# Forgetting heads' keys in the first attention steps, early gate rows, raw latents turned, X and the unit matrix first

## The chip, the cores and the metric

The kernel runs on one core of one Trainium2 chip. The time of a run is the device time of one execution in microseconds; of the kernel before three runs are given. Beside them stands one profiled execution, whose times of instructions and transfers are quoted below. The device time is a little longer than the span from the first to the last profiled instruction.

## What is computed

Three transformer layers in a row on 256 tokens of 1024 channels, all in fp32. Cut to its outline:

```
x = x + diff_attention(rms_norm(x) ...)        # 8 heads, two softmax maps each, head norm, w_out
x = x + hier_moe(rms_norm(x) ...)              # router, 64 experts (1024 -> 256 -> 1024), top 2
x = x + mla_attention(rms_norm(x) ...)         # latents: a = h @ w_a; rms_norm(cq) @ w_qb, rms_norm(ckv) @ w_kvb
x = x + hier_moe(rms_norm(x) ...)              # 64 other experts
mod = silu(c) @ w_ada + b_ada                  # sh1, sc1, ga1, sh2, sc2, ga2
x = x + ga1 * hybrid_mixer(modulate(rms_norm(x), sh1, sc1))   # 8 sliding heads, 8 forgetting heads
x = x + ga2 * conv_glu_mlp(modulate(rms_norm(x), sh2, sc2))
return rms_norm(x) * g_final
```

A forgetting head adds the difference of cumulated log sigmoids to its scores; a sliding head adds a slope by distance and a sink.

## The kernel before

Tokens stand in two tiles of 128. The kernel is written by hand: each engine has its own program in the order in which its lines call it, and semaphores join them (the blocks `sync`, `gpsimd`, `scalar`, `vector` and `tensor` at the end). SyncE's queue issues nearly all weight transfers, in units of 1 MB, into a ring of 12 slots and, for the experts, 4 more slots in the buffer BC; a unit's transfer waits until TensorE has released the slot (`load_unit` L230, `load` of the experts L1584).

The stages and their names: norm `n1`, projection `p1` (L486), turn `t1` (L556), first attention `a1` with output product `o1`; experts `m1`; norm `n2`, latents `pa`, turn of the latents `t3`, projections `pq` and `pkv` with the head norms of `heads_vector`, turns `t4q` and `t4k`, second attention `a2` with `o2`; experts `m2`; norm `n3`, projection `pz`, the channels `channels_tensor` (L1862), attention `a3` with `o3`; norm `n4` and the MLP (L2084, L2099).

`attention_stage` goes through 16 steps, 8 head pairs of the first token tile and 8 of the second. In step i TensorE forms the scores of step i+2 or i+3 (L627), turns the probabilities of step i (L638), does what the stage puts beside it, and multiplies with the values (L650). VectorE masks and stores (L684, L718), ScalarE takes the exponential (L744) and copies the turned map (L755). Beside them:

- A filler: in `a1` the products of the conditioning vector (L966), one unit in each of the first 8 steps. ScalarE copies the result (L978) and sends it to DRAM (L980) in step 7, and TensorE waits for that copy (`bank_read`) at the end of step 7.
- `OutStage`: in the second half of the steps TensorE multiplies the first tile's heads with w_out, in 16 pieces (L391), so many in each step as `counts` says, after the heads have been turned (L363) and ScalarE and VectorE have copied them (L372, L376). The second tile's product (L403) comes after the stage; the next norm's turn (L272) stands between its halves. VectorE adds the product to X (`add`).

The experts' transfers begin when the attention before has stored its last head (`x_free`); they pass some 200 MB per layer. At the latents, ScalarE copies a (L1648) and squares it (L1658), GpSimd takes the roots (L1668), VectorE scales the latents (L1674) and TensorE then turns them (L556). The head norms' VectorE loop starts with L1750.

In the third layer `channels_tensor` forms seven groups f = 0 to 6 of keys and queries; groups 5 and 6 are the keys of the forgetting heads, which steps 4 to 7 and 12 to 15 use. The rows of the first gate ga1 and their bias are loaded by GpSimd (L2013, L2014) after `a3` has stored its last head, and added by VectorE (L2018):

```
        def gate1_gpsimd(pool):
            a3.ready(pool)
            gate_gpsimd(pool, 0)
```

At the start TensorE waits for the unit matrix and both norm gains (`first`), which stand in SyncE's queue behind X.

Of the kernel before, what the change touches and what calls it, by code (L numbers as in the profile page):

```python
# [14 lines left out]
P = 128  # L15
# [86 lines left out]
def build(nc, t, out):  # L102

    with ExitStack() as ctx:
# [212 lines left out]
        def close_vector(dve, products, norm):  # L317
            products.add(dve, 0, 0)
# [13 lines left out]
        def close_vector_late(dve, products, norm):  # L332
            products.add(dve, 0, 0)
# [12 lines left out]
        class OutStage:  # L346
# [37 lines left out]
            def pieces(self, pe, first, last):  # L384

                for k in range(first, last):
                    g, n, c = k // 8, k // 4 % 2, 4 * (k // 8) + k % 4
                    self.heads_in(pe, 0, c)
                    u, view = self.blocks[n][1][g][0:2]
# [27 lines left out]
            def tensor(self, pe, i, heads_ready):  # L417

                if self.heads_norm:
# [4 lines left out]
                    counts = (0, 0, 0, 3, 3, 3, 2, 1)  # L424
# [21 lines left out]
            def vector(self, dve, i):  # L446
# [145 lines left out]
        def attention_stage(name, ready, heads, scale, bias, out, filler=None, mix=False, sink=0, squares=None,  # L592
                            turned_in=pT, heads_ready=None):
# [23 lines left out]
            def tensor(pe):  # L617
                ready(pe)

                def score(i):  # L620
                    tt, h, w = place(i)
                    if i >= ahead:
                        pe.wait_ge(*masked(maps * (i - ahead + 1)))
                    for m in range(maps):
# [31 lines left out]
                if filler:  # L656
                    filler.tensor(pe, 0)
                for i in range(items):
# [17 lines left out]
            def vector(dve):  # L676
# [48 lines left out]
                for i in range(items):  # L725
# [4 lines left out]
                    if i + 1 < items:  # L730
                        weigh(i + 1)
                    out.vector(dve, i)
# [3 lines left out]
            def scalar(act):  # L736
# [22 lines left out]
                for i in range(items):  # L759
# [3 lines left out]
                    if filler and i < HEADS:  # L763
                        filler.scalar(act, i)
                    if squares and i >= 1:
# [16 lines left out]
        def start_sync(sp):  # L782
# [35 lines left out]
        N_SMALL = 16 * 23  # L818
        first = sem("first")
        N_FIRST = 16 * 3  # L820
        x_in = [sem(f"x_in{tt}") for tt in range(TT)]

# [10 lines left out]
        n1 = norm_stage(lambda eng, tt: eng.wait_ge(*x_in[tt](16)), gains[:, 0, 0, :], extra=[(first, N_FIRST)],  # L833
# [816 lines left out]
        a_sq, a_rs, a_scaled = shared("sum_sq", 4), shared("sum_rs", 2), shared("sum_out", 2)  # L1650
# [676 lines left out]
```

## Time and profile before

| | us |
|---|---|
| median of 3 runs | 1658.75 (1657.42 to 1659.88) |
| profiled execution | 1659.99 |
| its span | 1658.3 |
| TensorE busy in it | 1378.7 (83%) |
| VectorE, ScalarE, GpSimd busy | 565.6, 260.4, 102.6 |
| mean granted TensorE clock | 0.921 of 2.4 GHz |
| bytes moved | 512.76 MB |

The span divides thus: the first attention up to its last stored head 0 to 152; experts 152 to 646; latents and second attention up to the last stored head 764; experts to 1255; hybrid attention to 1418; MLP to the end. The profiled execution is 1.2 us above the median. Busy shares of TensorE count an instruction at 1.2 GHz as busy for twice as long as at 2.4.

### The profile page before, as it was taken

Reading aid. Unit: us, or ns where it says so; the run is one execution under the profiler, and the core shown is the slowest. Engines: PE = TensorE matmul, PEld = TensorE weight load, DVE = VectorE, ACT = ScalarE, POOL = GpSimd, SP = SyncE. Lnnn points to the kernel's source line nnn. Section 1 sums busy time; section 2 is a strip of 40 time slices with the busy share of each in tenths; the row PEclk is TensorE's granted clock in tenths of the full one; section 3 lists DMA queues with packets and bytes.
Section 4 is the critical chain, followed back from the end, with each engine's and each line's share of the span. In section 5 each row is a group of like instructions: output and inputs, shape, how many; then the busy total and the mean of one; then the engine's idle time right before and its main releaser. Section 6 shows DMA issues by size and latency. Waiting matters only on the chain.

```text
span 1658.3 us, 24316 instructions
## 1 busy us (share of the span) xinstructions
PE 1378.7 (83%) x9354; PEld 840.2 (51%) x9354; DVE 565.6 (34%) x1490; ACT 260.4 (16%) x736; POOL 102.6 (6%) x191
## 2 busy tenths in 40 slices
PE   7989998677676667879997776767768988999998
PEld 3445555344443343555563443434435865788843
DVE  3444543122122222562632221222213133477721
ACT  2143211001010011353110010100101032111100
POOL 1312000000000001210100000000000032000000
PEclk9998999888898899999998888988988979999999
DMA  8763999999999999615999999999999512444400
GB/s 296 286 248 139 396 422 420 421 421 422 422 422 422 422 421 386 205 52 215 415 420 421 421 422 421 422 422 422 422 421 360 163 52 79 165 152 153 152 0 26
DMA packets 117188, 512.76 MB, mean 309 GB/s; under 512 B 11856, under 2 KB 46604, under 8 KB 64888
## 3 DMA queue, kind: packets, MB, share of 16 engines
q1 hardware_dynamic: 115504, 507.56, 77.0%
q0 software_dynamic: 1584, 4.13, 0.7%
q8 instruction: 51, 0.84, 0.2%
q14 instruction: 25, 0.20, 0.0%
q10 hardware_dynamic: 24, 0.02, 0.0%
HBM read 510.61 MB, written 1.07 MB: 309 GB/s over the span
## 4 chain that ended last, share of the span: by engine, by line
PE 33%; DMA 13%; SPq 6%; DVE 3%; issue 1%; ACT 1%; POOL 0%; DVEq 0%; POOLq 0%; ACTq 0%
DMA ring<-in_moe_w_up 13%; PE bank L2084 9%; SPq L1584 6%; PE bank L2099 5%; PE bank L1184 4%; PE bank L1862 3%; PE bank L391 2%; PE bank L650 1%; PE bank L403 1%; PE bank L1170 1%; PE bank L1199 1%; PE bank L627 1%; PE bank L486 1%; PE bank L1212 1%; PE bank L638 1%
## 5 line engine op out<-in xcount | busy, mean ns | idle before, releaser
L1184 PE MATMUL bank<-ring,hT 128*32 128x256 f32 (+1 forms) x3072 | 235.1, 463 | 161.3 <-DMA ring<-in_moe_w_up 106.2
L1184 PEld LDWEIGHTS bank<-ring,hT 128*32 128x32 f32 (+1 forms) x3072 | 136.6, 133 | 269.7 <-issue 236.1
L1435 DVE TENSOR_SCALAR pT<-pT 128x256 f32<-128x256 f32 x34 | 10.0, 294 | 475.4 <-ACT pT L1551 475.4
L2084 PE MATMUL bank<-hT,ring 128*128 128x256 f32 (+1 forms) x736 | 152.7, 370 | 1.7 <-ACT hT L285 1.7
L2084 PEld LDWEIGHTS bank<-hT,ring 128*128 128x128 f32 x736 | 134.9, 190 | 19.1 <-DVE hT L290 1.8
L486 PE MATMUL bank<-ring,hT 128*128 128x512 f32 (+4 forms) x352 | 124.7, 517 | 8.8 <-DVE hT L288 3.9
L1170 PE MATMUL bank<-A,hn 128*128 128x128 f32 x1088 | 127.8, 276 | 0.7 <-DVE A L1356 0.7
L1184 PE MATMUL bank<-BC,hT 128*32 128x256 f32 (+1 forms) x1024 | 85.9, 476 | 50.8 <-DMA BC<-in_moe_w_up 30.0
L1170 PEld LDWEIGHTS bank<-A,hn 128*128 128x128 f32 x1088 | 125.1, 193 | 3.2 <-issue 3.2
L1212 PE MATMUL bank<-A 128*128 128x512 f32 x256 | 118.4, 605 | 0.0
L486 PEld LDWEIGHTS bank<-ring,hT 128*128 128x128 f32 x352 | 65.8, 198 | 65.7 <-issue 53.1
L1184 PEld LDWEIGHTS bank<-BC,hT 128*32 128x32 f32 (+1 forms) x1024 | 48.8, 139 | 90.9 <-issue 78.8
L1199 PE MATMUL bank<-ring,gtab 128*32 128x512 f32 (+1 forms) x768 | 94.7, 595 | 0.0
L1551 ACT ACTIVATE pT<-bank 128x256 f32<-128x256 f32 x34 | 13.0, 383 | 513.6 <-PE bank L1184 513.6
L1212 PEld LDWEIGHTS bank<-A 128*128 128x128 f32 x256 | 46.0, 189 | 59.0 <-issue 59.0
L2099 PE MATMUL bank<-ring,BC 128*128 128x512 f32 x176 | 75.7, 592 | 0.0
L1378 DVE TENSOR_TENSOR hT<-bank,gains 128x512 f32<-128x512 f32 x34 | 23.5, 692 | 136.7 <-PE bank L1170 136.7
L256 POOL TENSOR_SCALAR stat<-stat 128x1 f32<-128x1 f32 x12 | 2.3, 190 | 986.5 <-ACT hn L249 986.5
L1436 DVE RECIPROCAL pT<-pT 128x256 f32<-128x256 f32 x34 | 59.6, 1753 | 1.2
L1540 ACT ACTIVATE hT<-bank,gains 128x128 f32<-128x128 f32 x136 | 38.7, 367 | 118.0 <-PE bank L1170 118.0
L2099 PEld LDWEIGHTS bank<-ring,BC 128*128 128x128 f32 x176 | 33.5, 190 | 41.6 <-issue 41.6
L1199 PEld LDWEIGHTS bank<-ring,gtab 128*32 128x32 f32 (+1 forms) x768 | 24.9, 112 | 49.5 <-issue 38.6
(289 smaller groups left out, 1478.5 us busy)
## 6 DMA issues: line engine op xcount, KB each, us to landing
ring<-in_moe_w_gate SPq DMA_DIRECT2D x100, 1024.0 KB, 24.8
ring<-in_moe_w_down SPq DMA_DIRECT2D x96, 1024.0 KB, 26.6
ring<-in_moe_w_up SPq DMA_DIRECT2D x92, 1024.0 KB, 26.6
BC<-in_moe_w_up SPq DMA_DIRECT2D x36, 1024.0 KB, 26.8
BC<-in_moe_w_down SPq DMA_DIRECT2D x32, 1024.0 KB, 26.2
BC<-in_moe_w_gate SPq DMA_DIRECT2D x28, 1024.0 KB, 26.1
ring<-in_w_ada SPq DMA_DIRECT2D x24, 1024.0 KB, 5.8
ring<-in_w_up SPq DMA_DIRECT2D x22, 1024.0 KB, 5.3
```

The costliest lines, as they stand in the source:

```text
L391: i = nc.tensor.matmul(bank[2 + n][:, :], hT[:, c, 0:P], view(slot(u))[:, c % 4, :], start=(c == 0), stop=(c == DC - 1))
L486: i = nc.tensor.matmul(ps(n, tt)[:, 0:w], lhs(seen + c, tt), view(slot(u))[:, c, :], start=(seen + c == 0), stop=(seen + c == total - 1))
L1170: i = nc.tensor.matmul(TOKENS[c // 4][:, c % 4 * P:(c % 4 + 1) * P], tokens_by_channel[:, tt, c, :], hot[:, tt, :], start=(tt == 0), stop= ...
L1184: i = nc.tensor.matmul(GATE[q * cap:(q + 1) * cap, part * FF:(part + 1) * FF], xg[:, c, q * cap:(q + 1) * cap], u[:, c, :], start=(c == 0) ...
L1199: i = nc.tensor.matmul(SIDE[nb][q * cap:(q + 1) * cap, :], hidT[:, c, q * cap:(q + 1) * cap], u[:, c, nb * NB:(nb + 1) * NB], start=(c == ...
L1212: i = nc.tensor.matmul(bank[2 * tt + nb][:, :], share[:, tt * P:(tt + 1) * P], yrow[:, nb * NB:(nb + 1) * NB], start=first, stop=False)
L1436: wait(nc.vector.reciprocal(e, e))
L1540: i = nc.scalar.activation(xg[:, c, :], TOKENS[1][:, (c - 4) * P:(c - 3) * P], ACT.Identity, scale=gain[:, c:c + 1])
L1584: sp.dma_start(slot(u), expert_src).then_inc(unit_full[s].sem, 16)
L1862: i = nc.tensor.matmul(bank[(2 + f) % 4][:, b * S:(b + 1) * S], w[:, c, b * P:(b + 1) * P], hT[:, c, :], start=(c == 0), stop=(c == DC - 1))
L2084: i = nc.tensor.matmul(bank[n % 4][:, b * S + t0:b * S + t1], w[:, c, b * P:(b + 1) * P], hT[:, c, t0:t1], start=(c == 0), stop=(c == DC - 1))
L2099: i = nc.tensor.matmul(bank[4 + 2 * tt + n][:, :], hidT3[:, 2 * j + c, tt * P:(tt + 1) * P], w[:, c, n * NB:(n + 1) * NB], start=(j == 0 a ...
```

## The change

- SyncE's queue begins with the unit matrix and X's first tile, then the attention gains and two weight units, then X's second tile. The FFN gains come after four units. TensorE waits for the unit matrix and X's first tile alone, and multiplies a cleared part of hT twice before that.
- `a1`: the pieces of the first tile's product are spread as (2, 2, 0, 2, 2, 2, 1, 1) in place of (0, 0, 0, 3, 3, 3, 2, 1); TensorE waits for the copy of the conditioning row in step 10 in place of step 7.
- The first `add` of each output product is done in step 15 of the attention.
- The latents are turned as they are; the root is applied in ScalarE's copies of the products (L1700 and following). VectorE's `latent_vector` is gone.
- Groups 5 and 6 of the channels are formed in four blocks, one before step 0 and one in each of steps 0 to 2 of `a3`; `channels_evac` of them stands in ScalarE's step 0 and VectorE's step 2.
- The first gate's rows and the convolution's are loaded before `bias_gpsimd`, in other places of BC, and added by VectorE before `a3`.

```diff
@@ OutStage.tensor, vector; close_vector
-        def close_vector(dve, products, norm):
-            products.add(dve, 0, 0)
+        def close_vector(dve, products, norm, first_added=True):
+            if not first_added:
+                products.add(dve, 0, 0)
...
-                    counts = (0, 0, 0, 3, 3, 3, 2, 1)
+                    counts = (2, 2, 0, 2, 2, 2, 1, 1)
...
+                if i == 2 * HEADS - 1:
+                    self.add(dve, 0, 0)
@@ attention_stage
+                    if beside:
+                        beside.keys_ready(pe, i)
...
+                if beside:
+                    beside.tensor(pe, 0)
...
-                    if filler and i + 1 == HEADS:
+                    if filler and i == HEADS + 2:
                         filler.bank_read(pe)
+                    if beside:
+                        beside.tensor(pe, i + 1)
@@ start_sync
-            for tt in range(TT):
-                ld(X[:, tt, :], x[:, tt, :], x_in[tt])
-            ld(ident, t["constants"][:, 0:P], first)
+            ld(ident, t["constants"][:, 0:P], x_in[0])
+            ld(X[:, 0, :], x[:, 0, :], x_in[0])
             ld(gains[:, 0, :, :], t["attn_norm"].rearrange("l (p c) -> p l c", c=DC), first)
-            ld(gains[:, 1, :, :], t["ffn_norm"].rearrange("l (p c) -> p l c", c=DC), first)
-            for u in range(4):
+            for u in range(2):
                 load_unit(sp, u)
+            ld(X[:, 1, :], x[:, 1, :], x_in[1])
+            for u in range(2, 4):
+                load_unit(sp, u)
+            ld(gains[:, 1, :, :], t["ffn_norm"].rearrange("l (p c) -> p l c", c=DC))
@@ the latents
-        t3 = turn_stage("t3", lambda pe: pe.wait_ge(*a_scaled(1)),
+        t3 = turn_stage("t3", lambda pe: pe.wait_ge(*pa.copied(2)),
...
-                        fill_ready=lambda pe, f: pe.wait_ge(*a_scaled(1 if f == 0 else 2)))
+                        fill_ready=lambda pe, f: pe.wait_ge(*pa.copied(2 if f == 0 else 4)))
...
+            eng.wait_ge(*a_rs(1))
+            return nc.scalar.activation(q_l[:, tt, 2 * n:2 * n + 2, :], ps.rearrange("p (h d) -> p h d", h=2), ACT.Copy,
+                                        scale=stat[:, 448 + tt:449 + tt])
@@ the hybrid attention
+        class ForgetKeys:
+            def tensor(self, pe, i):
+                if i < 4:
+                    f = 5 + i // 2
+                    if i % 2 == 0:
+                        z_left(pe, f - 4 if f == 5 else 4)
+                    channel_block(pe, f, i % 2)
+            def scalar(self, act, i):
+                if i == 0:
+                    channels_evac(act, 5)
+            def vector(self, dve, i):
+                if i == 2:
+                    channels_evac(dve, 6)
+            def keys_ready(self, pe, h):
+                if h == SWA_PAIRS:
+                    z_left(pe, 5)
+                if h == SWA_PAIRS + 2:
+                    z_left(pe, 6)
...
-            z_left(pe, 5)
-            z_left(pe, 6)
+            z_left(pe, 3)
+            z_left(pe, 4)
...
-            a3.ready(pool)
+            m2.ready(pool, 1)
             gate_gpsimd(pool, 0)
...
+            gate1_gpsimd(pool)
             bias_gpsimd(pool)
-            gate1_gpsimd(pool)
@@ vector, tensor
+            nc.vector.memset(hT[:, 0:2, :], 0.0).then_inc(cleared.sem, 1)
...
             forget_vector(dve)
+            gate_vector(dve, 0)
             a3.vector(dve)
-            gate_vector(dve, 0)
...
-            pe.wait_ge(*first(N_FIRST))
+            pe.wait_ge(*cleared(1))
+            for _ in range(2):
+                nc.tensor.matmul(bank[7][:, :], hT[:, 0, 0:P], hT[:, 0:2, :].rearrange("p c s -> p (c s)"), start=True, stop=True)
```

How the change moves instructions is shown at three places; the rows stand in each engine's own order.

SyncE at the very start, before (X, the unit matrix as konst, gains, weight units as ring):

```order
L785 DMA X<-in_x 128x1024 x2
L785 DMA konst<-in_constants 128x128
L785 DMA gains<-in_attn_norm 128x2x8
L785 DMA gains<-in_ffn_norm 128x2x8
L230 DMA ring<-in_diff_w_in 128x4x512 x4
```

and now:

```order
L801 DMA konst<-in_constants 128x128
L801 DMA X<-in_x 128x1024
L801 DMA gains<-in_attn_norm 128x2x8
L230 DMA ring<-in_diff_w_in 128x4x512 x2
L801 DMA X<-in_x 128x1024
L230 DMA ring<-in_diff_w_in 128x4x512 x2
L801 DMA gains<-in_ffn_norm 128x2x8
```

The first unit stands behind three transfers in place of five, and the second tile of X behind two units.

TensorE from the spreading of the gates (L1949) into the steps of `a3`, before (L1862 channels, L627 scores, L638 turn, L650 product with the values):

```order
L1949 MATMUL bank<-A,konst 128x256 x8
L1862 MATMUL bank<-hT,ring 128x256 x32
L627 MATMUL bank<-BC 128x128 x6
L638 MATMUL bank<-konst,BC 128x128 x2
L650 MATMUL bank<-A,BC 128x64 x2
L627 MATMUL bank<-BC 128x128 x2
L638 MATMUL bank<-konst,BC 128x128 x2
L650 MATMUL bank<-A,BC 128x64 x2
```

and now (the same lines are L1996, L1875, L635, L646, L658):

```order
L1996 MATMUL bank<-A,konst 128x256 x8
L635 MATMUL bank<-BC 128x128 x4
L1875 MATMUL bank<-hT,ring 128x256 x8
L635 MATMUL bank<-BC 128x128 x2
L646 MATMUL bank<-konst,BC 128x128 x2
L1875 MATMUL bank<-hT,ring 128x256 x8
L658 MATMUL bank<-A,BC 128x64 x2
L635 MATMUL bank<-BC 128x128 x2
L646 MATMUL bank<-konst,BC 128x128 x2
L1875 MATMUL bank<-hT,ring 128x256 x8
L658 MATMUL bank<-A,BC 128x64 x2
```

The 32 matmuls that stood ahead of all scores stand in four blocks of 8, the first behind the scores of steps 0 and 1, the others between turn and product of steps 0, 1 and 2.

GpSimd in the third layer, now (constants for `a3`, then the gate rows from mod_scratch and b_ada, the convolution's rows, and then the first biases; before, the four rows from mod_scratch to in_conv_b stood behind all biases):

```order
L1944 DMA A<-in_constants 128x128
L1945 DMA A<-in_constants 128x384
L2060 DMA BC<-mod_scratch 128x1024
L2061 DMA BC<-in_b_ada 128x1024
L2103 DMA BC<-in_conv_w 44x128 x3
L2104 DMA BC<-in_conv_b 44x128
L2037 TENSOR_SCALAR BC<-A 128x128 x8
```

Six DMA issues were moved ahead of the biases of the 16 steps.

## Rows read from the trace of the kernel before

**Rows 1.** The page's 40 slices of the span: DMA share in tenths

```profile
DMA  8763999999999999615999999999999512444400
```

**Rows 2.** Timeline of the first 40 us: start us, us, engine, line, operation, idle before it

```profile
6.86 1.97 PE L272 MATMUL bank<-konst,X 128*128 128x128 f32 x8 [6.86 <-DMA gains<-in_ffn_norm]
...
10.32 8.70 PE L486 MATMUL bank<-ring,hT 128*128 128x512 f32 x16 [1.49 <-DMA ring<-in_diff_w_in]
```

**Rows 3.** Line L230 in the first 12 us: its four weight units

```profile
DMA to landing us min/median/max: 7.0/10.2/13.4
```

**Rows 4.** Timeline of the first attention, steps 7 and 8, several engines

```profile
123.15 1.06 ACTq L980 DMA_DIRECT2D mod_scratch<-modrow  x1
123.18 1.11 PE L363 MATMUL bank<-konst,hn 128*128 128x128 f32 x4 [1.98 <-ACT modrow L978]
...
124.62 0.67 ACT L372 ACTIVATE hT<-bank,small 128x512 f32<-128x512 f32 x1
```

**Rows 5.** Windows: TensorE busy, weight loads, VectorE, ScalarE, GpSimd, clock, DMA share, GB/s

```profile
50.00:80.00 30.00, 30.00 (x71) 13.31 (x70) 14.85 (x27) 4.60 (x8) 10.08 (x9) 1.00 0.70 269
...
122.00:124.00 2.00, 0.82 (x4) 0.82 (x5) 0.68 (x2) 1.12 (x5) 0.00 (x0) 0.69 1.00 422
...
136.00:138.00 2.00, 2.00 (x8) 1.07 (x7) 1.50 (x7) 1.24 (x5) 0.03 (x1) 0.90 0.00 0
```

**Rows 6.** Timeline: scores in steps 12 and 13, first expert transfers, second tile's product

```profile
139.68 0.70 PE L627 MATMUL bank<-BC 64*128 64x256 f32 x4
...
143.71 0.70 PE L627 MATMUL bank<-BC 64*128 64x256 f32 x4
...
152.56 1.06 SPq L1584 DMA_DIRECT2D BC<-in_moe_w_gate  x2
...
155.85 7.03 PE L403 MATMUL bank<-ring,hT 128*128 128x512 f32 x16
```

**Rows 7.** Timeline of the latents, from ScalarE's second copy to the head norms

```profile
673.19 0.73 ACT L1648 ACTIVATE hn<-bank,stat 128x192 f32<-128x192 f32 x2 [2.78 <-PE bank L486]
...
676.62 1.55 PE L556 MATMUL bank<-konst,hn 128*128 128x128 f32 x6 [3.02 <-DVE hn L1674]
...
678.75 13.42 PE L486 MATMUL bank<-ring,BC 128*128 128x384 f32 x35 [0.58 <-DVE BC L572]
...
686.38 0.55 DVE L1750 TENSOR_REDUCE stat<-hn 128x2 f32<-128x384 f32 x1 [7.01 <-ACT hn L1726]
...
690.51 0.55 DVE L1750 TENSOR_REDUCE stat<-hn 128x2 f32<-128x384 f32 x1
```

**Rows 8.** Window of 1 us there, columns as in rows 5

```profile
682.00:683.00 1.00, 1.00 (x4) 0.55 (x3) 0.00 (x0) 0.00 (x0) 0.00 (x0) 0.73 0.00 0
```

**Rows 9.** TensorE's timeline from the last channel groups to step 9 of the hybrid attention

```profile
1323.00 15.77 PE L1862 MATMUL bank<-hT,ring 128*128 128x256 f32 x64
...
1345.40 1.11 PE L650 MATMUL bank<-A,BC 128*128 128x64 f32 x4 [0.47 <-ACT BC L755]
...
1348.34 1.11 PE L650 MATMUL bank<-A,BC 128*128 128x64 f32 x4 [0.47 <-ACT BC L755]
...
1369.59 0.70 PE L627 MATMUL bank<-BC 64*128 64x256 f32 x4
```

**Rows 10.** Windows of 1 us: hybrid attention's begin; second attention's steps, columns as in rows 5

```profile
1344.00:1345.00 1.00, 0.93 (x7) 0.50 (x6) 0.59 (x4) 0.73 (x6) 0.92 (x3) 0.87 0.02 8
...
730.00:731.00 1.00, 0.76 (x6) 0.76 (x7) 0.22 (x2) 0.57 (x3) 0.00 (x0) 1.00 0.00 0
```

**Rows 11.** Timeline of the hybrid attention's end: gate rows, adds, norm

```profile
1395.60 0.60 POOL L2013 DMA_DIRECT2D A<-mod_scratch  x1 [14.70 <-DVE hn L718]
...
1401.17 1.23 DVE L2018 TENSOR_TENSOR A<-A 128x1024 f32<-128x1024 f32 x1 [3.26 <-DMA A<-in_b_ada]
...
1408.21 1.97 PE L272 MATMUL bank<-konst,hn 128*128 128x128 f32 x8 [4.16 <-DVE hn L262]
1409.98 8.53 PE L403 MATMUL bank<-ring,hT 128*128 128x512 f32 x16
```

More of the change, by code:

```diff
@@ L330, in close_scalar, with close_vector_late @@
                 norm.evac(act, tt, 1)
-        def close_vector_late(dve, products, norm):
-            products.add(dve, 0, 0)
+        def close_vector_late(dve, products, norm, first_added=True):
+            if not first_added:
+                products.add(dve, 0, 0)
             products.add(dve, 0, 1)
@@ L592, in attention_stage @@
         def attention_stage(name, ready, heads, scale, bias, out, filler=None, mix=False, sink=0, squares=None,
-                            turned_in=pT, heads_ready=None):
+                            turned_in=pT, heads_ready=None, beside=None):
             st = Stage()
@@ L731, in vector @@
                         weigh(i + 1)
+                    if beside:
+                        beside.vector(dve, i)
                     out.vector(dve, i)
@@ L764, in scalar @@
                         filler.scalar(act, i)
+                    if beside:
+                        beside.scalar(act, i)
                     if squares and i >= 1:
@@ L816, in start_sync @@
             assert n_loaded[0] == N_SMALL
-        N_SMALL = 16 * 23
+        N_SMALL = 16 * 24
         first = sem("first")
-        N_FIRST = 16 * 3
+        N_FIRST = 16
         x_in = [sem(f"x_in{tt}") for tt in range(TT)]
+        cleared = sem("cleared")
         w_in = t["diff_w_in"][0]
@@ L831, in have_small @@
             eng.wait_ge(*loaded(N_SMALL))
-        n1 = norm_stage(lambda eng, tt: eng.wait_ge(*x_in[tt](16)), gains[:, 0, 0, :], extra=[(first, N_FIRST)],
+        n1 = norm_stage(lambda eng, tt: eng.wait_ge(*x_in[tt](16 * (2 - tt))), gains[:, 0, 0, :], extra=[(first, N_FIRST)],
                         late_root=True)
@@ L1850, in z_left, with channel_bank, channel_block @@
             eng.wait_ge(*(z_out_a if f % 2 else z_out_v)(f // 2 + 1))
+        def channel_bank(f):
+            return bank[(2, 3, 0, 1, 2, 3, 2)[f]]
+        def channel_block(pe, f, b):
+            u = turned_units[f]
+            unit_here(pe, u)
+            w = wide_unit(slot(u))
+            for c in range(DC):
+                i = nc.tensor.matmul(channel_bank(f)[:, b * S:(b + 1) * S], w[:, c, b * P:(b + 1) * P],
+                                     hT[:, c, :], start=(c == 0), stop=(c == DC - 1))
+            if f == 0 or b == 1:
+                i.then_inc(unit_done.sem, 1)
         def channels_tensor(pe):
-            for f, u in enumerate(turned_units):
+            for f in range(5):
                 if f < 4:
@@ L1857, in channels_tensor @@
                     z_left(pe, f - 4)
[L1858 to L1859 removed]
                 for b in range(1 if f == 0 else 2):
[L1861 to L1864 removed]
+                    channel_block(pe, f, b)
                 if f in (2, 3, 4):
                     (forget_sums, forget_turn, forget_spread)[f - 2](pe)
+        class ForgetKeys:
[16 more added lines that the diff above has]
+                    z_left(pe, 6)
+        forget_keys = ForgetKeys()
         def channels_evac(eng, f):
             eng.wait_ge(*unit_done(turned_units[f] + 1))
[L1870 removed]
+            ps = channel_bank(f)
             copy = (lambda dst, src: nc.scalar.activation(dst, src, ACT.Copy)) if f % 2 else nc.vector.tensor_copy
@@ L2022, in add @@
                 xs = X[:, tt, n * NB:(n + 1) * NB]
-                product = scratch[k][:, n * NB:(n + 1) * NB]
+                product = scratch[k][n]
                 dv.done(nc.vector.tensor_tensor(product, ps, gate_rows[k][:, n * NB:(n + 1) * NB], ALU.mult))
@@ L2239, in _ @@
             forget_scalar(act)
-            for f in (1, 3, 5):
+            for f in (1, 3):
                 channels_evac(act, f)
```

43 lines of the change are left out of this document (15 added, 28 removed).

## The prediction, on record before the change was timed

> **What bounds the kernel now.** I read the page's slices first. The DMA queues are full in slices 5 to 16 and 20 to 30, the two expert layers [rows 1]: there the 200 MB of a layer set the end, and nothing that TensorE does faster is worth time. Outside them, from 10 to 152 us, from 646 to 764 and from 1255 to the end, the DMA rows are low and TensorE's timeline is nearly closed. So a microsecond taken from TensorE's order before 152 or 764 counts if it lets the expert transfers start earlier. They start right behind the last stored head: the first issue is at 152.56 [rows 6], and the DMA queues stand idle before it. So I read the chain of waits of these three stretches and the granted clock beside it, and look in each for gaps of TensorE and for work at 1.2 GHz in place of 2.4.
>
> **The change part by part**, summed against the profiled execution (1659.99, 1.2 above the median).
>
> *Start.* TensorE begins at 6.86, released by the FFN gains, and the first product at 10.32, released by a weight unit [rows 2], which needs 7.0 us from its issue to its landing [rows 3]. The unit is now issued behind three small or half-size transfers and not five, two issues of about 0.45 us each earlier, and has 0.5 MB less ahead of it, some 1.2 us at about 400 GB/s. I take 2.0 us. X's first tile and the turn come sooner still and no longer bound it. The first product's 16 records take 8.70 us, where the same 16 take 7.03 later [rows 2, 6]: the clock is at 1.2 GHz in the beginning, which costs 1.7. The two products on cleared data warm it, but then TensorE waits again for the unit; I count half, 0.8. Start: −2.8, bounds 0 and −4.5. The projection behind it leaves TensorE no gap (30.00 us busy of 30 from 50 to 80 [rows 5]), so this goes through.
> The Trainium skill, "TensorE: Matmul & The Clock Gate", section "HAM oscillation — how this bites in real kernels", and its first part say that the low clock is spent by time at work and not by the number of matmuls, and that a gap can bring it back. By the first half of that alone this term would be −3.7 and the sum 28.7; no row here shows a warmed start.
>
> *First attention.* In step 7 TensorE stands 1.98 us for ScalarE's copy of the conditioning row [rows 4]; by the shares of two windows the clock falls at 122.8 and comes back at 136.4 [rows 5]. That wait moves to step 10, where the copy is long done. But what is late next stands in the same queue: ScalarE issues a transfer (1.06 us from 123.15) and copies the turned heads only until 125.3 [rows 4]. The pieces, now in step 8, wait for that copy, about 2.0 us from 123.3. From there at 2.4 GHz: a step with three pieces takes 4.03 [rows 6], a piece 7.03/8 = 0.88, so a step with two takes 3.15. Step 8 ends at 127.6, step 9 at 130.8, step 10 (no piece, but the turn of four heads) at 133.0; step 13 begins at 139.3 and not at 143.71. From there to the first expert transfer it was 8.85; two pieces fewer make 7.1, so 146.4: −6.1. As the gap is as long as before, the clock most likely falls again, now with TensorE closed behind it, so for 4 to 5 us: +2.3. I take −3.8, bounds 0 (the gap only moves and the clock stays down as before) and −6.1. The `add` put into VectorE's step 15 (0.7 us) fits ahead of the last head's product and costs nothing; without that cover, 0.7.
>
> *Latents.* ScalarE's second copy ends at 673.92; TensorE turns only at 676.62, after 3.02 us for squares, root and scaling, and pq begins at 678.75 [rows 7]. Now the turn goes at 674.1, its copies end at about 675.8, and pq begins at 675.9. The clock falls in that gap and returns at 682.5, by the window's share [rows 8]. So pq's first block ran 3.8 us at half clock; its 12 records, 384 columns wide, take 0.33 each at 2.4 GHz (three quarters of 7.03/16), 3.9 in all, and 5.8 with the low stretch, to 684.6. With the clock kept it ends at 679.8. VectorE's loop, begun at 686.38 and then closed at 4.13 per round [rows 7], sets the end of this stage; it begins 5.0 earlier with the clock kept and 2.9 earlier without. The two gaps left (0.5 and 1.0) speak for kept more often than not: −4.5. The scale in ScalarE's copies is free: L1648 has one too.
>
> *Hybrid attention.* The last two groups run as one stretch of 15.77 until 1338.8, and step 9 begins at 1369.59: 30.8 us for steps 0 to 8 [rows 9]. The clock falls at 1344.7 [rows 10], and a step then takes 2.94, 0.47 of it waiting [rows 9]. In the new order TensorE first waits 0.8 for the last copies of the forget rows, and forms two scores (0.7). Steps 0 to 2 have a block of 3.9 each between turn and product and so no gap: 1.33 each of their own, 4.0. Steps 3 to 7 are open: 2.47 of work at 1.2 GHz is 1.23 at 2.4, and with waits 2.0 each, the last two with wider scores 2.2: 10.4. Step 8 with eight turns 2.95. Together 18.9, so −11.9 with the clock kept. It was kept in the second attention at 0.76 busy [rows 10], about what these steps have. I take off 2 for the copies of both groups, which stand in ScalarE's step 0 and VectorE's step 2 ahead of the next copy and store: −10, bounds −5 (clock down from step 4 to 8) and −11.9. Queues: GpSimd has six more issues, 3.7 us, in the 55 us in which it waits before its first bias; VectorE's gate addition (1.23) [rows 11] delays mask 0, covered by the first block. The 1 MB more of transfers then go beside weights for which TensorE doesn't wait; without that slack 3 us.
>
> *Gate rows.* After the last head GpSimd issues them at 1395.60, VectorE adds them at 1401.17, and TensorE, done with its product at 1404.05, turns at 1408.21 after 4.16 idle, at half clock [rows 11]: 8 turns take 1.97 for 1.05, the next product 8.53 for 7.03. All of it goes: without the load the chain of add, square, root and scale ends at 1402.4, before the product. −4.2 −0.9 −1.5 = −6.6; bounds −5 and −7. Late next is the second tile's chain, as before.
>
> Sum: −2.8 −3.8 −4.5 −10 −6.6 = −27.7. 1659.99 − 27.7 = 1632.3; 1.2 lower against the median, **1631**.
>
> **Rivals.** *B: the clock falls again in the open steps.* For it: it fell in this very attention after gaps of under 1 us [rows 10], and it fell at each gap of 2 us or more that I read closely. Against: the second attention's steps. Price: the hybrid term at its bound, 5 less, and the latents at theirs, 1.6 less: 1638. The page named above says the same in general: without activity TensorE is throttled.
>
> *C: what lies before the expert layers is hidden by them.* The next transfers after the first four wait for slots that the output product frees. If these set the pace, the start, first attention and latents (11.1) are lost: 1642. Against it: the product follows the last head at the same distance, so the slots move along, and the queues are idle before 152.56 [rows 6].
>
> *D: slower.* The four blocks go into a stretch whose clock was low. If it falls at the steps' begin and the steps keep it down, the blocks take 31.5 and not 15.8, and the second eight steps with their pieces, some 26 us at 2.4 GHz, as long again: +15.7 + 26, and the gain of 10 is gone: 1631 + 52 = 1683. It decides from the point where the first scores of the stage run at 1.2 GHz and no later product lifts them. Against it: the clock came back before step 9 once TensorE was closed, and a step with a block is closed.
>
> *E: the change doesn't do what it says*, as when a wait of a later semaphore sends TensorE to the same place: no gain, 1659. The order of the instructions shows the blocks and loads moved.
>
> **How the numbers follow.** Forecast (clock kept in most open stretches) 0.5; B 0.35; C 0.08; D 0.03; E and the rest 0.04. The range: down to 1625, where all terms but one stand at their far bounds (−33 to −34); up to 1645, which takes in B with a start and a first attention at little, and C. Faster means by over 0.2%, 3.3 us, about what a measurement here can tell: forecast, B and C, and some of the rest, 0.95; same 0.02; slower 0.03.
>
> **What would show it.** In the profile of the changed kernel: the first L492 product near 8.3; the first expert transfer near 146; 0.5 us of gap before the latents' second turn and the first round of the head norms 9 to 12 us earlier than 686 in all; the clock at 2.4 in steps 3 to 7 of the hybrid attention; no gap of TensorE between the two halves of its output product. I am wrong if the expert layers take longer than before, if a gap of 2 us or more stands ahead of the pieces in every attention, or if the hybrid steps 3 to 7 take 2.9 each.

## The result, and the profile after

The changed kernel takes 1633.12 us (median of 4 runs, 1631.00 to 1634.69); the kernel before, beside it on the same chip, 1659.32. The ratio is 0.9838, with a 95% interval of 0.9821 to 0.9855: 26 us faster, where 28 were forecast. The profiled execution took 1634.69, the slowest of the four; its span is 1632.9 (before 1658.3), TensorE's mean granted clock 0.930 (before 0.921), the bytes are the same 512.76 MB.

The page's slices of the span, clock and DMA share in tenths:

```profile
PEclk9999999888898898999999898898888989999999
DMA  8765999999999999615999999999999721644400
```

The full slices of the two expert layers are as many as in [rows 1], but a slice of 41 us can't size changes of a few. So I cut each trace at four marks that stand in every kernel and compare the pieces: TensorE's turn of X's second tile (start), the issue of the first expert transfer (first attention), that of the second layer's (experts and latents), and GpSimd's first root of the third norm (experts).

| stretch (us) | before | after | moved | forecast |
|---|---|---|---|---|
| to the second turn | 18.86 | 19.87 | +1.0 | −2.8 |
| to the first expert transfer | 133.70 | 127.88 | −5.8 | −3.8 |
| to the second layer's | 611.29 | 606.16 | −5.1 | −4.5 (latents) |
| to the third norm's root | 495.56 | 494.69 | −0.9 | 0 |
| to the end | 398.89 | 384.30 | −14.6 | −16.6 (hybrid, gates) |

TensorE's timeline of the start, and two windows of it (columns as in rows 5):

```profile
1.55 3.78 PE L2326 MATMUL bank<-hT 128*128 128x512 f32 x4 [1.55 <-DVE hT L2297]
5.25 1.16 PE L272 MATMUL bank<-konst,X 128*128 128x128 f32 x8
10.24 9.79 PE L492 MATMUL bank<-ring,hT 128*128 128x512 f32 x16 [3.84 <-DMA ring<-in_diff_w_in]
```

```profile
9.00:10.00 1.00, 0.00 (x0) 0.00 (x0) 0.00 (x0) 0.00 (x0) 0.00 (x0) 0.50 1.06 412
15.00:16.00 1.00, 1.00 (x2) 0.27 (x1) 0.00 (x0) 0.27 (x2) 0.56 (x2) 0.67 1.06 391
```

The two products at 1.55 do raise the clock: the turn takes 1.16 and not 1.97 [rows 2]. But the first weight unit, issued at 2.24, releases TensorE at 10.24, as late as before, and in the 3.84 us of waiting the clock falls again. It is back only in the window 15 to 16, and the first product takes 9.79, more than the 8.70 of [rows 2].

The first attention, TensorE and SyncE's queue, and a window in the gap:

```profile
123.79 0.44 PE L646 MATMUL bank<-konst,BC 128*128 128x128 f32 x2
126.36 1.99 PE L395 MATMUL bank<-ring,hT 128*128 128x512 f32 x4 [2.13 <-ACT hT L374]
147.75 0.85 SPq L1603 DMA_DIRECT2D BC<-in_moe_w_gate  x2
```

```profile
125.00:126.00 1.00, 0.00 (x0) 0.00 (x0) 0.49 (x2) 0.67 (x3) 0.18 (x1) 1.00 0.99 418
```

The gap of [rows 4] has moved one step on and is as long as before, but here the clock holds through it: two pieces take 1.99.

The latents (TensorE, then VectorE's head norms):

```profile
668.44 1.18 PE L562 MATMUL bank<-konst,hn 128*128 128x128 f32 x6 [0.37 <-ACT hn L1667]
670.19 15.75 PE L492 MATMUL bank<-ring,BC 128*128 128x384 f32 x48 [0.58 <-DVE BC L578]
676.13 0.55 DVE L1765 TENSOR_REDUCE stat<-hn 128x2 f32<-128x384 f32 x1 [5.33 <-ACT hn L1741]
```

The gap of 3.02 in [rows 7] is 0.37, and VectorE's loop begins 10.25 us earlier, at 676.13.

The hybrid attention, from its first scores to step 9, and its end:

```profile
1312.81 1.23 PE L635 MATMUL bank<-BC 64*128 64x128 f32 x8 [0.88 <-DVE A L1969]
1313.97 4.78 PE L1875 MATMUL bank<-hT,ring 128*128 128x256 f32 x16
1319.37 3.62 PE L1875 MATMUL bank<-hT,ring 128*128 128x256 f32 x16
...
1333.92 0.66 PE L658 MATMUL bank<-A,BC 128*128 128x64 f32 x4 [0.47 <-ACT BC L769]
...
1335.85 0.66 PE L658 MATMUL bank<-A,BC 128*128 128x64 f32 x4 [0.47 <-ACT BC L769]
1336.43 0.67 PE L635 MATMUL bank<-BC 64*128 64x128 f32 x4
...
1341.55 1.11 PE L658 MATMUL bank<-A,BC 128*128 128x64 f32 x4 [0.47 <-ACT BC L769]
...
1350.92 0.70 PE L635 MATMUL bank<-BC 64*128 64x256 f32 x4
...
1378.36 7.03 PE L407 MATMUL bank<-ring,hT 128*128 128x512 f32 x16
1385.23 1.05 PE L272 MATMUL bank<-konst,hn 128*128 128x128 f32 x8
1386.12 7.03 PE L407 MATMUL bank<-ring,hT 128*128 128x512 f32 x16
```

and a window in step 5:

```profile
1336.00:1337.00 1.00, 1.00 (x8) 0.74 (x8) 0.29 (x1) 0.56 (x4) 0.92 (x2) 0.81 0.94 316
```

A block takes 3.62 and covers a step's waits; the first takes 4.78, as the clock was down from about 1312.7 to 1316. The open steps 3 and 4 (products 1333.92 and 1335.85) run at 2.4 GHz, 1.93 apart; at about 1336.6 the clock falls. Counted from the scores at their begin, step 5 takes 2.80, the steps 6 and 7 take 3.36 each, and step 8 with its eight turns takes 4.97, together 14.49. Step 9 begins at 1350.92, 18.7 us earlier than in [rows 9], 11.1 of which was won before the stage. The end has no gap where [rows 11] had 4.16, and the second half of the product takes 7.03 and not 8.53: from the last turn of heads (1377.92; 1396.59 before) to the MLP's first matmuls (1393.08; 1418.44 before) it is 15.2 for 21.9.

### The profile page after: what moved, and what is told of

The parts are those of the page before. It is cut to its first block, busy times and chain, and to the rows that moved or that the text cites. A ratio compares the mean times of both kernels' runs of the same rounds, so it can differ in the third digit from the quotient of the medians.

```text
span 1632.9 us, 24329 instructions
## 1 busy us (share of the span) xinstructions
PE 1367.9 (84%) x9358; PEld 833.6 (51%) x9358; DVE 564.5 (35%) x1487; ACT 263.2 (16%) x736; POOL 103.5 (6%) x191
## 2 busy tenths in 40 slices
DMA packets 117188, 512.76 MB, mean 314 GB/s; under 512 B 11856, under 2 KB 46604, under 8 KB 64888
## 4 chain that ended last, share of the span: by engine, by line
PE 35%; DMA 11%; SPq 7%; DVE 2%; issue 1%; ACT 1%; POOL 0%; POOLq 0%; DVEq 0%; ACTq 0%
DMA ring<-in_moe_w_up 11%; PE bank L2131 9%; SPq L1603 6%; PE bank L2146 5%; PE bank L1203 4%; PE bank L1875 3%; PE bank L1189 2%; PE bank L1218 2%; PE bank L395 2%; PE bank L407 2%; PE bank L1231 2%; PE bank L635 1%; PE bank L492 1%; PE bank L658 1%; PE bank L646 1%
## 5 line engine op out<-in xcount | busy, mean ns | idle before, releaser
L1203 PE MATMUL bank<-ring,hT 128*32 128x256 f32 (+1 forms) x3072 | 243.0, 476 | 162.2 <-DMA ring<-in_moe_w_up 100.8
L492 PE MATMUL bank<-ring,hT 128*128 128x512 f32 (+4 forms) x352 | 125.4, 519 | 11.1 <-DVE hT L288 3.9
L1203 PE MATMUL bank<-BC,hT 128*32 128x256 f32 (+1 forms) x1024 | 76.8, 434 | 49.8 <-DMA BC<-in_moe_w_up 32.6
```

Of the source, the lines that this page charges most:

```text
L492: i = nc.tensor.matmul(ps(n, tt)[:, 0:w], lhs(seen + c, tt), view(slot(u))[:, c, :], start=(seen + c == 0), stop=(seen + c == total - 1))
L1203: i = nc.tensor.matmul(GATE[q * cap:(q + 1) * cap, part * FF:(part + 1) * FF], xg[:, c, q * cap:(q + 1) * cap], u[:, c, :], start=(c == 0) ...
```

## The experiments

All are edits of the changed kernel except `before_fill`. The table has each trace cut at the same marks; the last column is the median of the runs (4 each, `before_fill` 10). The runs come from four groups on two chips; the kernel before, timed again in each, had medians of 1659.3, 1657.5, 1659.9 and 1658.0, so a difference of under 2 us between two medians says little.

| kernel | second turn | to 1st transfer | to 2nd | to root | to end | median |
|---|---|---|---|---|---|---|
| before | 18.86 | 133.70 | 611.3 | 495.6 | 398.9 | 1659.3 |
| before_fill | 20.96 | 132.41 | 610.5 | 494.0 | 393.4 | 1652.9 |
| after | 19.87 | 127.88 | 606.2 | 494.7 | 384.3 | 1633.1 |
| u_ends | 19.38 | 129.50 | 606.3 | 494.9 | 391.4 | 1642.2 |
| u_keys | 17.57 | 127.87 | 606.5 | 494.1 | 396.9 | 1643.6 |
| u_latents | 17.63 | 129.51 | 611.1 | 494.2 | 386.0 | 1638.0 |
| u_counts | 16.86 | 131.22 | 608.3 | 494.9 | 384.6 | 1638.1 |
| u_read | 15.48 | 128.93 | 606.1 | 494.1 | 386.0 | 1635.6 |
| bridge | 17.64 | 129.56 | 606.3 | 494.5 | 384.2 | 1633.7 |
| late_row | 20.02 | 126.44 | 606.1 | 496.1 | 384.5 | 1632.5 |
| fill | 17.51 | 129.51 | 604.3 | 494.3 | 380.6 | 1629.4 |
| ahead_fill | 20.30 | 127.86 | 606.5 | 494.5 | 383.5 | 1634.2 |
| joined | 16.53 | 126.43 | 605.9 | 494.2 | 379.7 | 1624.6 |
| joined_spread | 16.96 | 126.41 | 606.7 | 494.7 | 379.2 | 1624.5 |

**Undoing parts.** `u_ends`: the old order of loads and no early products; the gates' loads and VectorE's sum behind the attention, and with them the hybrid attention's first `add`. Of its edit, the line of the gates:

```diff
-            gate1_gpsimd(pool)
             bias_gpsimd(pool)
+            gate1_gpsimd(pool)
```

> The changed kernel with both its ends undone: SyncE's old order at the start and no products ahead of the first turn; the gate rows loaded after the last head and added to VectorE's work behind the attention. By the traces (start 1.0 us worse with the change, gates 6.7 better): 1633.1 - 1.0 + 6.7 = 1638.8, and the second turn at 18.9 us as before the change. By the forecast's terms (start 2.8 better, gates 6.6): 1642.5.

Measured 1642.21 (ratio to before 0.9893, 0.9876 to 0.9909). That is the 1642.5 of the forecast's terms, but not for their reasons, as the start shows. The gap is back in TensorE's timeline, and with it 7.1 us in the last column:

```profile
1391.14 1.97 PE L272 MATMUL bank<-konst,hn 128*128 128x128 f32 x8 [4.12 <-DVE hn L262]
```

The start is 0.5 better than in the one trace of after. The rest of the 8.5 us between the two traces is in the first attention: the same gap of 2.13 cost the clock here, and its stretch is 129.50 for 127.88. So the gates with that `add` are worth 7, and one trace doesn't size the start.

`u_keys`: `for f in range(7)` in `channels_tensor`, and nothing beside the attention.

> The changed kernel with the last two groups of keys formed ahead of the hybrid attention again, in one stretch, as before the change; the rest stays. Theory (the blocks fill the gaps of the first steps and keep the clock up through the first five of them): step 9 begins 7.5 us later than in the changed kernel, 1640.6. Rival (the hybrid stage won by what else changed there: the add in VectorE's last step, fewer waits ahead of the first scores): under 3 us, 1636. If the clock happens to fall later in the open steps than it did in the one trace of before: 1638.

Measured 1643.62, 10.5 more than after and 3.0 more than expected. In the last column it is 12.6 more; the clock fell at about 1330.6 and came back only at about 1361, in the steps with pieces, later than in the kernel before (windows):

```profile
1360.00:1361.00 1.00, 1.00 (x2) 0.34 (x1) 0.56 (x3) 1.00 (x4) 0.92 (x3) 0.50 0.00 0
1361.00:1362.00 1.00, 1.00 (x3) 0.38 (x2) 0.00 (x0) 0.54 (x3) 0.77 (x2) 0.84 0.00 0
```

Confirmed in kind; the size depends on when the clock returns.

`u_latents`: VectorE scales, and the turn waits for it.

> The changed kernel with the latents scaled by VectorE before they are turned, as before the change. Theory (the 2.6 us chain of squares, root and scaling and the clock that fell in its gap): the second attention's first expert transfer comes 4.4 us later, and as the expert layer behind it only shifts, 1637.5. If the clock holds through the 3 us of gap this time: 2.9 us, 1636. Rival (the expert layer's transfers take up what is won ahead of them): 1633.

Measured 1637.98, where 1637.5 was expected; the column that holds the latents is 611.1, that of before to 0.2 us. (In the traces with the new order of the latents it lies between 604.3 and 608.3.) The expert layer behind it takes as long as ever (494.2), so the rival that transfers hide the gain is out. TensorE's timeline, with the gap of [rows 7]:

```profile
670.48 1.49 PE L562 MATMUL bank<-konst,hn 128*128 128x128 f32 x6 [3.01 <-DVE hn L1693]
672.55 11.87 PE L492 MATMUL bank<-ring,BC 128*128 128x384 f32 x28 [0.58 <-DVE BC L578]
```

`u_counts` and `u_read` take apart the first attention's change:

```diff
-                    counts = (2, 2, 0, 2, 2, 2, 1, 1)
+                    counts = (0, 0, 0, 3, 3, 3, 2, 1)
```
```diff
-                    if filler and i == HEADS + 2:
+                    if filler and i + 1 == HEADS:
```

> The changed kernel with the pieces of the first attention's output product spread as before, (0, 0, 0, 3, 3, 3, 2, 1); TensorE's wait for the conditioning row stays in step 10. Measured from TensorE's turn of X's second tile to the first expert transfer, the kernel before took 133.7 us, the changed one 127.9 where its clock held and 129.5 where it fell in the gap of 2.13. Theory (the three steps without pieces leave TensorE open after the filler has ended, and that kept the clock down before): 131 to 133, so 1635 to 1637. Rival (the wait in step 7 alone brought it down; without it and without pieces that wait for the heads' copy there is no gap of 2 us at all): 126.5 to 128, 1632.

> The changed kernel with TensorE's wait for the conditioning row back in step 7, the pieces spread as now. The heads are then turned 1.5 us later, but ScalarE copies them only behind the row's transfer anyway. Theory (the gap only moves from step 8 to step 7 and the pieces behind it close TensorE either way): the stretch from the second turn to the first expert transfer is 127.9 or 129.5 us as in the changed kernel, at most 1 more, 1633 to 1634. Rival (the gap in step 7 weighs more, as in the kernel before): 131 to 133, 1636 to 1638.

Measured 1638.08 and 1635.61, 1.1 and 1.6 us above their theories, the second close to its rival's 1636. The stretches, 131.22 and 128.93, say what the medians blur (their runs lie 6.5 and 5.8 us apart), and both are where the theory put them. Without pieces in steps 8 to 10 the wait moves to the product of step 8, the clock falls at about 124.5 and the open steps behind it run at 1.2 GHz (TensorE's timeline of `u_counts`):

```profile
123.64 0.71 PE L658 MATMUL bank<-A,pT 128*128 128x128 f32 x4 [2.42 <-ACT pT L769]
124.28 1.08 PE L635 MATMUL bank<-BC 64*128 64x256 f32 x4
...
126.45 1.23 PE L658 MATMUL bank<-A,pT 128*128 128x128 f32 x4 [0.47 <-ACT pT L769]
```

With the wait back in step 7 the clock falls as well, but pieces follow, it is back at 124, and the stretch is no longer than in other traces with a fall. So the spread of the pieces carries 1.7 to 3.3 us of this part; moving the wait gave nothing measurable once they are spread, as ScalarE's row and its transfer stay ahead of the heads' copy. The 1.2 to 2.5 us between `u_counts` and the two traces with the old attention (132.41 and 133.70) are left to the moved wait and the early `add`; no run parts these two.

The four medians with a part undone lie 9.1, 10.5, 4.9 and 5.0 us above that of after, 29.5 in all where the whole change gave 26.2: the parts account for the gain, and their sum is no closer than the runs scatter.

**The start.** `bridge` adds, behind `n1.turn(pe, 0)`:

```diff
+            for _ in range(4):
+                nc.tensor.matmul(bank[0][:, :], ident, X[:, 0, 0:NB], start=True, stop=True)
```

> The changed kernel (1633.1) with four products of the unit matrix with X's first tile behind the first turn, in the 3.84 us in which TensorE stands for the first weight unit. Theory (the two products at the very start raise the clock and the gap behind the turn drops it again, so the first projection product runs at 1.2 GHz for longer than it did before the change): the clock stays at 2.4, the first product takes 7.0 to 7.3 us in place of 9.8, the second turn comes 2.5 to 2.8 us earlier, and the time is 1630.4. Rival (the weight units and X's second tile set the pace of the first 20 us): under 1 us is won, 1632.5. If a clock once raised at 1.5 us doesn't hold through four short products either: no gain, 1633.1 or up to 1 more.

TensorE's timeline, start and first attention:

```profile
6.12 3.60 PE L2329 MATMUL bank<-X,konst 128*128 128x512 f32 x8
10.69 7.11 PE L492 MATMUL bank<-ring,hT 128*128 128x512 f32 x16 [0.98 <-DMA ring<-in_diff_w_in]
...
124.11 3.68 PE L395 MATMUL bank<-ring,hT 128*128 128x512 f32 x4 [2.13 <-ACT hT L374]
```

The mechanism held: 7.11 for the product, the turn 2.2 earlier, though the unit landed late. The median did not move (1633.72, where 1630.4 was expected). The trace shows one reason: in this execution the clock fell in the attention's gap, two pieces took 3.68, and the stretch is 1.7 longer than in the one trace of after.

How much the start varies shows in a trace of another kernel with the changed start (`fill`), where the unit landed 1.4 us earlier and the clock was soon back (timeline):

```profile
8.87 8.80 PE L492 MATMUL bank<-ring,hT 128*128 128x512 f32 x16 [2.43 <-DMA ring<-in_diff_w_in]
```

Over all traces the second turn came at 18.86, 20.96 and 19.38 with the old order (mean 19.7) and at 15.48 to 20.30 with the new one (8 traces, mean 18.2); bridged at 17.64, 16.53 and 16.96 (17.0). In `u_read`, the 15.48, the unit was there before the copies, the gap was 1.35 and the clock was up in the whole product (7.11); there the turn had still taken 1.97, at 1.2 GHz. So the two early products raise the clock at the turn in some executions only: it takes 1.15 to 1.97 over the eight.

**The first attention's gap.** `late_row` puts ScalarE's copy of the conditioning row and its transfer behind `out.scalar(act, i)` in step 7.

> The changed kernel with ScalarE's copy of the conditioning row and its transfer put behind the copy of the turned heads in step 7 of the first attention. TensorE stood 2.13 us for that copy of the heads, and in three of four traces with this very gap the clock fell in it or right behind it for about 3 us. Theory: the gap shrinks to 0.5 us, the clock stays in every execution, the first expert transfer is issued at 145 to 146 in place of 147.0 to 147.75, and the time is 1.6 us shorter than an execution whose clock held, 3 us shorter than one whose clock fell: 1630.5. Rival (VectorE's or the next exponentials' chain is as late as that copy): nothing won, 1633.

TensorE's timeline in step 8:

```profile
124.73 1.98 PE L395 MATMUL bank<-ring,hT 128*128 128x512 f32 x4 [0.35 <-ACT hT L374]
```

The gap is 0.35, the stretch 126.44: 1.4 shorter than 127.9, 3.1 shorter than 129.5. The median, 1632.50, gained only 0.6 and is 2 above the expected 1630.5, less than its runs differ (5.0); in the profiled run the second expert layer took 1.5 us longer than in the others, which I can't explain. In `joined` and `joined_spread` the stretch is 126.4 again.

**The open steps.** `fill` adds to `ForgetKeys.tensor`, for steps 3 to 7:

```diff
+                elif i <= 8:
+                    for _ in range(2):
+                        nc.tensor.matmul(bank[3][:, 0:P], ident, ident, start=True, stop=True)
```

> The changed kernel with two products of the unit matrix with itself (128 columns) between turn and product of each of the steps 3 to 7 of the hybrid attention; their results are read by nobody. Theory (the clock falls because the open steps leave TensorE idle for a quarter of the time): the clock stays, the steps 5 to 8 take 2.0 to 2.3 us in place of 3.4, step 9 begins 4 to 5.5 us earlier, 1628 to 1629. Rival (the clock falls there whatever small work is added, or the waits on ScalarE and VectorE set the step): the ten products cost up to 0.45 us each time two of them don't fit in a gap, 1633 to 1636.

TensorE's timeline, the first block and steps 7 to 9, and a window of these:

```profile
1310.95 6.34 PE L1875 MATMUL bank<-hT,ring 128*128 128x256 f32 x16
...
1340.59 0.66 PE L658 MATMUL bank<-A,BC 128*128 128x64 f32 x4
1341.18 0.70 PE L635 MATMUL bank<-BC 64*128 64x256 f32 x4
...
1344.19 0.70 PE L635 MATMUL bank<-BC 64*128 64x256 f32 x4
```

```profile
1340.00:1341.00 1.00, 0.97 (x9) 0.78 (x8) 0.93 (x6) 0.53 (x4) 0.53 (x2) 1.00 0.00 0
```

Measured 1629.38, 3.7 less than after, and 3.7 less in the last column. The small products fit into the waits, and the clock stays in all steps. The steps 5 to 8 take 9.2 us in place of 14.49; 1.6 of these 5.3 are lost again in the first block, where the clock came back later in this trace (6.34 for 4.78). The Trainium skill, "TensorE: Matmul & The Clock Gate", section "A second HAM failure mode: psum-queue depth-cycling", says that frequent short idles between groups of matmuls make the clock go down and up; the pair after and `fill` agrees, at 0.47 us of idle per step.

`before_fill` has the same two products in steps 0 to 7 of the kernel before.

> The kernel before (1659.3) with the same two products in each of the steps 0 to 7 of the hybrid attention, and nothing else changed. Theory (most of the 30.8 us of its steps 0 to 8 is the low clock): the steps take 1.9 to 2.2 us in place of 2.9, step 9 begins 9 to 12 us earlier, 1648 to 1650; then more could be had by keeping the clock than by moving the keys' blocks into the steps. Rival (the moved blocks won by filling gaps; the clock falls at the stage's begin anyway): the products add time, 1659 to 1664.

Measured 1652.93 (10 runs, 1645.85 to 1658.05; ratio 0.9969, 0.9953 to 0.9985), neither what the theory nor what the rival said. In its trace TensorE waited 0.99, 0.45 and 0.90 us up to the turn of step 0; the clock fell at about 1341.3, behind the first of the small products, and then stayed down for 13.6 us although TensorE was closed (windows, columns as in rows 5):

```profile
1341.00:1342.00 1.00, 1.00 (x8) 0.85 (x7) 0.58 (x4) 0.91 (x5) 0.88 (x3) 0.63 0.03 8
...
1348.00:1349.00 1.00, 1.00 (x7) 0.91 (x6) 0.59 (x5) 0.19 (x1) 0.06 (x1) 0.50 0.00 0
...
1354.00:1355.00 1.00, 1.00 (x7) 1.00 (x6) 0.59 (x5) 0.29 (x2) 0.18 (x1) 0.54 0.00 0
```

It came back at about 1354.9, in the same work. Over the ten runs the time follows the clock: the two fastest, 1645.85 and 1649.40, have mean clocks of 0.932 and 0.931, the two slowest, 1656.41 and 1658.05, 0.924 and 0.922. The theory's 1648 to 1650 is about where the two fastest lie.

`ahead_fill` closes these waits too (0.35 and 0.24 are left), in the changed kernel with the keys formed ahead.

> The changed kernel with the last two groups of keys formed ahead of the hybrid attention again, and TensorE kept at work with products of the unit matrix that nobody reads: four before the stage's first wait, six before step 0, two in each of the steps 0 to 7. It tells what moving the keys is worth where the clock holds either way. Theory (most of that part's gain was clock): 1629.4 (the changed kernel with small products) plus 2.9 for gaps that the blocks no longer fill, 1632.3, against 1643.6 for the same order without the small products. Rival (the blocks' place itself matters): 1637 or more. If the clock falls all the same in the stage's begin, as it did in one trace of the kernel before with small products: about 1640.

In its trace the clock holds from the long stretch of channels on (1.00 in every window from 1318), and the last column is 383.5: 2.8 more than `fill`, 13.4 less than `u_keys`. The median, 1634.15, is 1.9 over the expected 1632.3; its profiled run had the latest start of all, 20.30. With small products in either order, where the keys are formed is worth 2.8 us by these stretches and 4.8 by the medians; without them, 12.6 and 10.5. (Against `joined_spread` below, whose first block was as quick as in after, it is 4.3.)

**Together.** `joined` is `bridge`, `late_row` and `fill` in one.

> Three additions to the changed kernel in one: the four products behind the first turn, the conditioning row's copy behind the heads' copy, and the two small products in each of the steps 3 to 7 of the hybrid attention. If each gives what its own trace showed and they add up: 1 to 2 at the start, 2 to 3 in the first attention, 4 in the hybrid attention, 1625 to 1626. Rival (what is won ahead of the expert layers is lost in them): only the hybrid part is left, 1629.4.

Measured 1624.56 (1624.17 to 1626.05; ratio to before 0.9796, 0.9770 to 0.9823): 8.6 below the changed kernel, 0.4 better than expected, and the narrowest of all in its runs. Each stretch shows its part, 16.53, 126.43 and 379.7.

`joined_spread` puts four small products ahead of the stage's first scores.

> The joined kernel (1624.6) with four more small products between the spreading of the forget rows and the hybrid attention's first scores, in the 0.88 us for which TensorE waits for VectorE's copies. In every trace with the changed order the clock was down from that gap until within the first block, which took 4.8 to 6.3 us in place of 3.6. Theory (the gap brings it down): the block takes 3.6 and the time is 1.2 to 2.7 us shorter, 1622 to 1623. Rival (the spreading's products, which use 8 rows of the array, bring it down; the gap has no part in it): 1624.6 or up to 0.3 more.

Measured 1624.51, as the rival said, though runs 3.9 us apart can't tell it from the theory; the trace can. There is no gap left, and the clock falls all the same, behind the 16 products of the spreading, which contract over 8 of the 128 partitions, while the busy share is 1.00; the first block takes 4.76 and not 3.6 (timeline, then windows):

```profile
1304.50 3.71 PE L2001 MATMUL bank<-A,konst 8*128 8x256 f32 x16
1308.15 1.19 PE L2010 MATMUL bank<-konst 128*128 128x128 f32 x8
...
1310.42 4.76 PE L1877 MATMUL bank<-hT,ring 128*128 128x256 f32 x16
```


```profile
1308.00:1309.00 1.00, 1.00 (x9) 0.85 (x8) 0.83 (x3) 0.00 (x0) 0.00 (x0) 1.00 1.08 379
1309.00:1310.00 1.00, 1.00 (x9) 0.85 (x10) 1.00 (x1) 0.00 (x0) 0.96 (x1) 0.57 0.26 78
1310.00:1311.00 1.00, 1.00 (x7) 0.69 (x4) 0.38 (x3) 0.00 (x0) 0.92 (x2) 0.50 0.12 25
```

## Why the prediction was right, and where it was not

The time was forecast at 1631 and came out at 1633.1; the terms were less good than the sum. Of the signs named, the latents' gap, the head norms' begin and the closed output product came; the first product (9.79 for 8.3) and the clock in the steps 5 to 7 did not. Two slips in the working are too small to matter: the sum with the larger start is 28.6 and not 28.7, and by its own ends (684.6 and 679.8) the latents' bound is 4.8 and not 5.0.

**Start** (−2.8 forecast). The failed step is "I take 2.0 us" for the unit: its issue moved from 3.22 to 2.24, and where its landing released TensorE, that was at 10.3 and 10.9 with the old order and at 8.2 to 10.7 (mean of eight 9.6) with the new one: 1.0 earlier, what the issue gained, and scattered by more. The 1.2 for bytes ahead of it did not show. The half counted for a warm clock (0.8) gave about 0.1: the first product took 9.0 on average over the eight traces with the new order and no bridge, and 9.1 over the three with the old. The clock was raised and lost again in the wait, which I had named and then priced at half. The Trainium skill, "TensorE: Matmul & The Clock Gate", section "HAM oscillation — how this bites in real kernels", says that a gap can bring the low clock back. This decided, as the window 9 to 10 shows, and it did so in other traces behind shorter waits than that section has them, from 1.95 us on (`u_counts`). With most of the gap filled, `bridge` has 7.11. The second turn of the same eight traces against the three gives −1.6; the profiled one happened to be +1.0.

**First attention** (−3.8). Price and mechanism were both right, by halves: "the clock most likely falls again" was so in four of seven traces with this gap (stretch 129.5, −4.2), and in three it held (127.9, −5.8, near the bound of −6.1). Both are counted from the one trace of before; from `before_fill`, which is the same code up to there, they are −2.9 and −4.5. `u_counts` and `u_read` name the spread of the pieces as the main carrier.

**Latents** (−4.5). −5.1 and, undone, +4.9: the bound with the clock kept. Rival C is out: what was won ahead of the expert layers came through; the second layer's stretch stays within 494.0 to 496.1 in all fourteen traces, whatever came before it.

**Hybrid attention** (−10). −7.5. The mechanism of rival B took the difference: the clock held from the second block through two open steps and fell in the third, so the steps 5 to 8 took 14.5 and not the 9.35 forecast. What I read "in the second attention's steps" did not carry over, and "about what these steps have" was the failed step: these steps work 1.46 us of 1.93, the same share of 0.76, and it was no guide. In `fill`, with the clock held, the four steps take 9.2, as forecast. My cost of 2 for the copies was not there: TensorE's waits in these steps are the same 0.47 on the probabilities' copy.

**Gate rows** (−6.6). −6.7 between the two marks, 7.1 with both halves undone. Right as worked out. (The undone run also puts the first `add` back.)

The 0.9 of the second expert layer is not the change's: `before_fill` took 494.0 there.

The time lies in the range. That the sum came out near is in part a cancelling: start 3.8 worse and hybrid 2.5 worse in the profiled run, first attention 2.0 and latents 0.6 better, and 1 from the expert layers.

## What to carry to other kernels

Where TensorE sets the pace, price a wait twice: its length, and the work behind it at 1.2 GHz. Most of what moving the keys gave was clock (12.6 us alone, 2.8 with products that nobody reads in either order; 10.5 and 4.8 by the medians), so such filler products in waits of half a microsecond are the cheap first experiment. And when a stage's gain is below the scatter of the runs, cut several traces at the same marks and compare the stretch, not the total.

## What was not expected of the hardware

- One and the same gap lowers the clock in some executions and not in others: 2.13 us ahead of the pieces, four falls in seven traces, 1.6 us apart in the stretch. The Trainium skill, "TensorE: Matmul & The Clock Gate", section "What's actually happening", says of a kernel's start that its slow part varies from run to run; here it is seen in the middle of a kernel too.
- A run of narrow products may cost the clock like a wait: in all fourteen traces it fell 0.2 to 1.2 us behind the 16 products over 8 partitions, also where TensorE was busy throughout (`joined_spread`, `ahead_fill`). No run leaves these products out, so that it was their narrowness is argued and not shown. The clock fell there in the kernel before as well, unnoticed: the window 1325 to 1326 of its channels has a clock of 0.50, and that is why 64 records took 15.77 there and not twice 7.07.
- Work that keeps a clock up doesn't always bring it back: the filled steps held 2.4 GHz in `ahead_fill` and ran 13.6 us at 1.2 in `before_fill`, with busy shares of 0.98 and 1.00.
- The landing of the first weight unit scatters by 2.5 us between executions with one order of issues (8.2 to 10.7), more than the change of order moved it.
